# GpSimd keeps a running sum of the finished feature tiles for three layer-norm means of a two-layer backbone

## Chip, cores and metric

One core of a Trainium2 chip. The metric is the device time of one execution in microseconds (us). Engines are named as in the profile: PE (TensorE matmul), PEld (its weight load), DVE (VectorE), ACT (ScalarE), POOL (GpSimd), SP (SyncE, which issues most of the DMAs).

## The reference, cut to what matters

Two layers (DEPTH = 2) work on 512 latent and 128 context tokens of width 1024. Each layer is a mixer (attention and two recurrent groups) and then a channel mixer (SwiGLU in layer 0, top-2-of-8 experts in layer 1), each followed by a residual and a layer norm:

```
mix = mixer(...)                                  # ends in ... @ w_out[l]
x = layer_norm(alpha * x + g1 * mix, ln_g[l, 0], ln_b[l, 0])
x = layer_norm(alpha * x + g2 * channel_mixer(l, x * (1 + sc2) + sh2), ln_g[l, 1], ln_b[l, 1])

def layer_norm(x, g, b):
    mu = jnp.mean(xf, -1, keepdims=True)
    var = jnp.mean(jnp.square(xf - mu), -1, keepdims=True)
    return (xf - mu) * lax.rsqrt(var + NORM_EPS) * g + b
```

The change concerns `mu` in three of the four norms: after the mixer of layer 0, after the channel mixer of layer 0, after the mixer of layer 1. The last norm works on rows of tokens and is not touched.

## The kernel before, in words

The residual stream is held transposed in SBUF: `xT` has 128 partitions, KT = 8 feature tiles and NT = 640 tokens, float32, so `xT[:, m]` is one tile of 128 features x 640 tokens. The mean over features runs over partitions and over the eight tiles. PE makes it: a 128x128 matrix of the value 1/1024 (`mean`, a constant) times every tile, accumulated in one PSUM slot, which leaves the mean of each token in all 128 partitions. `average(i, k)` (line 2918) issues this for tile k of norm i: one call of `wide` (line 2330), a product of 512 and one of 128 columns; as these are float32, the trace shows two matmul instructions for each, four per tile. `variance(i)` (line 2927) does the same with the squared centred tiles, in four pieces of tokens.

**Norm 1 of each layer (mean1).** PE computes the output projection in eight parts wo0 to wo7 (`mixer`, lines 2891 to 2899), 48 f16 matmuls of 512 or 128 columns each. DVE adds each finished part to its tile of `xT` (line 2179, the stt helper at 1695, one instruction for the latent and one for the context columns), and frees the PSUM slot. Behind wo4 PE issues the mean's tiles 0 to 2, behind wo5 tile 3, behind wo6 tile 4 and behind wo7 tiles 5, 6 and 7 (lines 2938 to 2948). Each `average` waits for DVE's addition to that tile (`L.done`).

**Norm 2 of layer 0 (mean2).** The feed-forward network runs over 11 slabs of 256 hidden columns. In the last slab the second product `down(m, 1)` finishes output tile m, DVE adds it to `xT[:, m]` (line 2215). Behind tile 6 PE issues the mean's tiles 0 to 3, and behind tile 7 the tiles 4 to 7 (lines 2991 to 3002).

**Behind each mean.** DVE subtracts it in four pieces of tokens (line 1783), ACT squares (1473), PE sums the squares, ACT makes 1/sqrt (1453, 1454), DVE scales (1768), DVE and ACT modulate (1774, 1461), ACT and DVE split the result in two f16 halves (1467, 1780), and PE starts the next products piece by piece.

**GpSimd's order of work around the change.** POOL works through its own program in order: `lower` (line 827; the instruction is line 831) makes the low f16 half of a weight piece of 128x2048. In each layer the last of these are the four pieces wo0 to wo3 (lines 986 to 990); the stores of the new states go out behind wo1 (`send`, line 837). In layer 0 there follow the 11 slabs of `slab(i)` (line 995): three weight pieces each (line 1000) and two activation tiles (line 1003). Then layer 1 begins with `lower` of its pieces qa0 and qa1. SP fetches a weight piece into one of three buffers of `wbuf` when POOL has lowered the one before in it (lines 683 to 694 and 733). `out_done` counts the kernel's stores, six in each layer. `va` holds the value rows of the layer; its last part is a source of one of the stores (line 861).

Of the kernel before, what the change touches and what calls it, by code (L numbers as in the profile page):

```python
# [135 lines left out]
TURN_UNIT = {3: 2, 5: 3, 8: 4, 10: 5, 13: 6, 15: 7, 18: 8}  # L136
LAST_TURN = 9


# [149 lines left out]
def backbone_kernel(nc, x_prompt, x_sample, cache_k, cache_v, state_gdn, state_hgrn, c, c_ctx, w_mod, b_mod, w_in,  # L289
# [12 lines left out]
    with ctx:  # L302
# [153 lines left out]
        rsb = [mem(mix, 4 * CVW + CVW * i, CVW) for i in range(2)]  # L456
        vaf = va[:, :, :].rearrange("p t n -> p (t n)")
        osq, osqL, osqC = mem(spare, 0, 2, NT), mem(mix, 2048, 2, NT)[:, :, 0:LAT], mem(mix, 3328, 2, P)
        ors, orsL, orsC = mem(spare, 1280, NT), [mem(spare, 1280, LAT), vaf[:, 0:LAT]], mem(spare, 1792, 2, P)
# [5 lines left out]
        def mixed(i, k):  # L465
# [57 lines left out]
            "near_in wide_ready ltc_ready tt_ready t5_act t6_act ah_clear centred sq_ready rstd_ready scaled xn_ready v_in v_exp "  # L523
            "hot_ready m_hot g2_out zero_in id_ready x1_first x1_out picked_ready slots_ready tiles_ready gates_ready xs_out "
            "m_hi13 m_lo13 m_hi2 m_lo2 m_xt m_xhi m_xlo m_up m_silu m_act m_ahi m_alo m_turn m_at "
# [297 lines left out]
        def _(pool):  # L823
# [10 lines left out]
            def send(l, S, dst):  # L834

                for f in range(2):
                    pool.dma_start(heads_of(dst[0, l], f), head(S, f)).then_inc(sg["out_done"], 16)

            for l in range(DEPTH):
# [146 lines left out]
                for what in OUT_PIECES:  # L986
                    lower(l, what)
                    if what == "wo1":
                        L.done(f"{l}.hs4")
                        send(l, SH, new_sh)  # L990
                if l % 2:
                    continue
# [14 lines left out]
                L.made["w_lo"] = sbase + 3 * SLABS[l]  # L1007
                L.took["w_hi"] = sbase + 3 * SLABS[l]

            pool.wait_ge(sg["slots_ready"], 1)  # L1010
# [1297 lines left out]
        def _(pe):  # L2308
# [108 lines left out]
            for l in range(DEPTH):  # L2417
# [500 lines left out]
                def average(i, k):  # L2918

                    if i == 1:  # L2920
                        L.done(J(f"wo{k}"))
                    else:
                        pe.wait_ge(ps_free[k % 4], 3 * (SLABS[l] - 1) + base[k % 4] + 2 + k // 4)
                    s = ps[:, PS[J(f"mean{i}")][0]]
                    return wide(s, mean, xT[:, k], k == 0, k == KT - 1)

# [11 lines left out]
                for m in range(3, KT):  # L2938
                    open_(J(f"wo{m}"))
                    close(mixer(m, range(KT), lat + last), J(f"wo{m}"))  # L2940
                    if m == 4:
                        open_(J("mean1"))
                        for k in range(3):
                            average(1, k)
                    if m > 4:
                        average(1, m - 2)
                average(1, 6)
                close(average(1, 7), J("mean1"))
                variance(1)
# [4 lines left out]
                def slab(i, first=False, last=False):  # L2954
# [30 lines left out]
                    for m in range(KT):  # L2985
                        b = m % 4
                        if m >= 3:
                            pe.wait_ge(ps_free[b], i * 3 + (base[b] + 1 + m // 4))
                            down(m, 0)
                        down(m, 1).then_inc(ps_full[b], 1)  # L2990
                        if last and m == 6:
                            open_(J("mean2"))
                            for k in range(4):
                                average(2, k)

# [3 lines left out]
                slab(SLABS[0] - 1, last=True)  # L2999
                for k in range(4, KT):  # L3000
                    ins = average(2, k)
# [159 lines left out]
```

## Time and profile before

| | us |
|---|---|
| median of 3 runs | 2382.66 |
| lowest and highest of them | 2378.59, 2385.62 |
| span of the profiled execution (first to last instruction) | 2378.1 |
| PE busy in it | 2118.8 (89%) |
| DVE, ACT, POOL busy | 1449.5 (61%), 1283.3 (54%), 754.2 (32%) |

The profiled execution's own time is not listed apart from the three runs; its span stands 4.6 us under their median and 0.5 us under the lowest. A span leaves out what lies before the first and behind the last instruction. PE works nearly all the time, so a stage is to be read by what stands between its matmuls. A timeline row gives the start, the duration, the engine, the line, the operation, the output and input, the shape and the number of instructions merged in the row; in brackets the idle time of the engine before it and what ended it.

### The profile page before, as it was taken

To read this page: it belongs to the slowest core of one execution; us is meant where nothing else is said; L and a number is where in the kernel's file an instruction comes from. 1 tells how busy PE (TensorE), PEld (TensorE's weight loads), DVE (VectorE), ACT (ScalarE), POOL (GpSimd) and SP (SyncE) were. 2 spreads that over 40 slices of the span, in tenths; PEclk is the share of its full clock that TensorE was granted. 3 is DMA by queue.
4 is the path that set the end of the run, shared out by engine and by line. 5 is a ranking of instruction groups with operands and counts; after the bars stand their busy time and mean duration, and the time that the engine had idled before them with its cause. 6 is when DMAs were issued, how large, how long until landed. Compare 5 with 4: busy or idle time off the path is not lost.

```text
span 2378.1 us, 54636 instructions
## 1 busy us (share of the span) xinstructions
PE 2118.8 (89%) x23130; PEld 1305.1 (55%) x23130; DVE 1449.5 (61%) x1797; ACT 1283.3 (54%) x1665; POOL 754.2 (32%) x556
## 2 busy tenths in 40 slices
PE   5999787978989999999899878878869999999994
PEld 3756456745565555555675558645544444444442
DVE  3254656668261221215558667595379999999985
ACT  3443554556453333423543665465368877778763
POOL 0332115433404242423233236422023333333332
PEclk8999898988999999999999989998979999999997
DMA  9352680020303131315231000100456777990014
GB/s 285 121 174 77 212 285 28 4 58 8 106 17 106 53 106 53 106 53 166 77 103 39 1 10 4 41 21 22 140 223 223 238 265 276 330 335 34 36 65 183
DMA packets 215529, 278.48 MB, mean 117 GB/s; under 512 B 28321, under 2 KB 188941, under 8 KB 215183
## 3 DMA queue, kind: packets, MB, share of 16 engines
q1 hardware_dynamic: 203776, 243.60, 31.5%
q0 software_dynamic: 8432, 29.89, 3.4%
q8 instruction: 166, 2.72, 0.5%
q10 hardware_dynamic: 3103, 1.85, 0.3%
q14 instruction: 52, 0.43, 0.1%
HBM read 368.36 MB, written 29.11 MB: 167 GB/s over the span
## 4 chain that ended last, share of the span: by engine, by line
PE 53%; issue 16%; DVE 13%; POOL 8%; ACT 7%; DMA 2%; SPq 1%; POOLq 0%; DVEq 0%; ACTq 0%
PE ps L2328 50%; POOL mix L1000 6%; DVE mix L1695 1%; DVE arena L1687 1%; DVE mix L1687 1%; DMA wbuf<-in_w_mod 1%; POOL mix L1003 1%; DVE small L1910 1%; DVE arena L1691 1%; SPq L727 1%; DVE mix L1849 1%; DMA const<-in_w_mod 1%; ACT mix L1461 1%; PE ps L3097 1%; PE ps L3073 1%
## 5 line engine op out<-in xcount | busy, mean ns | idle before, releaser
L2328 PE MATMUL ps<-hT,mix 128*128 128x512 f16 (+2 forms) x3024 | 376.7, 287 | 25.0 <-DVE hT L1687 11.8
L2328 PE MATMUL ps<-w,xgT 128*128 128x512 f16 x1632 | 366.3, 381 | 5.3 <-DVE w L2228 5.3
L2228 DVE SCALAR_TENSOR_TENSOR w<-wst,w 128x2048 f16<-128x2048 f32 x136 | 309.8, 2318 | 25.6 <-ACT w L1558 25.5
L2328 PEld LDWEIGHTS ps<-hT,mix 128*128 128x128 f16 x3024 | 227.1, 99 | 172.9 <-issue 22.2
L1032 POOL TENSOR_TENSOR a<-aval,a 128x256 f16<-128x256 f32 x68 | 158.3, 2328 | 370.4 <-ACT a L1606 370.4
L2328 PEld LDWEIGHTS ps<-w,xgT 128*128 128x128 f16 x1632 | 157.7, 98 | 184.5 <-issue 9.6
L1558 ACT ACTIVATE w<-wst 128x2048 f16<-128x2048 f32 x136 | 251.5, 1898 | 9.6 <-DMA xs_rows<-htok,slot_i 9.6
L2328 PE MATMUL ps<-mix 128*128 128x512 f16 (+5 forms) x1856 | 204.7, 288 | 15.7 <-POOL mix L1003 8.8
L2328 PE MATMUL ps<-hT,arena 128*128 128x128 f16 (+1 forms) x1440 | 200.7, 300 | 1.1 <-DVE const L1687 1.1
L2328 PE MATMUL ps<-w2m,aT 128*128 128x512 f16 x816 | 187.2, 379 | 3.8 <-DVE aT L2266 3.8
L2328 PEld LDWEIGHTS ps<-mix 128*128 128x128 f16 (+3 forms) x1856 | 121.3, 123 | 90.4 <-POOL mix L1003 12.4
L2234 DVE SCALAR_TENSOR_TENSOR w2m<-wst,w2m 128x2048 f16<-128x2048 f32 x68 | 155.7, 2290 | 15.0 <-ACT w2m L1566 14.6
L2192 DVE SCALAR_TENSOR_TENSOR mix<-ps,mix 128x640 f32<-128x640 f32 x22 | 18.1, 825 | 238.6 <-PE ps L2328 238.6
L831 POOL TENSOR_TENSOR arena<-wbuf,arena 128x2048 f16<-128x2048 f32 x24 | 99.8, 4157 | 195.7 <-ACT arena L1063 195.6
L2328 PEld LDWEIGHTS ps<-hT,arena 128*128 128x128 f16 x1440 | 111.3, 98 | 88.0 <-issue 5.8
L1000 POOL TENSOR_TENSOR mix<-wbuf,mix 128x2048 f16<-128x2048 f32 x33 | 134.4, 4089 | 57.0 <-ACT mix L1510 56.8
L2328 PEld LDWEIGHTS ps<-w2m,aT 128*128 128x128 f16 x816 | 79.6, 98 | 100.2 <-DVE aT L2266 4.7
L1566 ACT ACTIVATE w2m<-wst 128x2048 f16<-128x2048 f32 x68 | 129.4, 1902 | 0.2 <-PE ps L2328 0.2
L2328 PE MATMUL ps<-arena 64*32 64x32 f32 (+5 forms) x4320 | 104.7, 219 | 22.0 <-issue 18.4
L1003 POOL TENSOR_TENSOR mix<-mix 128x640 f16<-128x640 f32 x22 | 30.7, 1396 | 256.8 <-ACT mix L1519 256.8
L2199 DVE TENSOR_TENSOR arena<-arena,ps 128x640 f32<-128x640 f32 x80 | 65.6, 821 | 73.7 <-PE ps L2328 73.7
L2328 PEld LDWEIGHTS ps<-arena 64*32 64x32 f32 (+3 forms) x4320 | 69.8, 116 | 54.1 <-issue 41.9
(359 smaller groups left out, 3546.3 us busy)
## 6 DMA issues: line engine op xcount, KB each, us to landing
wst<-in_moe_w SPq DMA_DIRECT2D x204, 1024.0 KB
wbuf<-in_w_mod SPq DMA_DIRECT2D x40, 1024.0 KB
wbuf<-in_ffn_w SPq DMA_DIRECT2D x33, 1024.0 KB
wbuf<-in_w_in SPq DMA_DIRECT2D x20, 1024.0 KB
xs_rows<-in_table SPq DMA_DIRECT2D x17, 512.0 KB, 6.4
ys_rows<-yb POOLq DMA_DIRECT2D x17, 512.0 KB, 4.2
wbuf<-in_w_out SPq DMA_DIRECT2D x32, 256.0 KB
xg<-xs_rows POOLq DMA_DIRECT2D x16, 512.0 KB, 5.5
```

The costliest lines, as they stand in the source:

```text
L727: sp.dma_start(o, i).then_inc(w_full[slot], 64 // len(parts))
L831: L.do(g.tensor_tensor(split_parts(what)[1], wpiece(WP[f"{l}.{what}"][0], n), split_parts(what)[0], ALU.subtract), "w_lo")
L1000: g.tensor_tensor(v[1], wpiece(j), v[0], ALU.subtract).then_inc(sg["w_lo"], 1)
L1003: g.tensor_tensor(a2[1][:, t], gbuf[:, t], a2[0][:, t], ALU.subtract).then_inc(sg["a_lo"], 1)
L1032: g.tensor_tensor(a16[:, s % 2, 1, :], aval[:, s % 2, :], a16[:, s % 2, 0, :], ALU.subtract).then_inc(sg["m_alo"], 1)
L1558: a.activation(quarter(s, p)[0], staged(s, p), ACT.Copy, scale=WS).then_inc(sg["m_hi13"], 1)
L1566: a.activation(w2p[s % 2][0], staged(s, 2), ACT.Copy, scale=WS).then_inc(sg["m_hi2"], 1)
L1687: ins = v_.tensor_tensor(o, x, y, op)
L2199: v_.tensor_tensor(yacc[:, m], yacc[:, m], ps[:, b, 0:NT], ALU.add).then_inc(ps_free[b], 1)
L2228: v_.scalar_tensor_tensor(out=q[1], in0=staged(s, p), scalar=WS, in1=q[0], op0=ALU.mult, op1=ALU.subtract).then_inc(sg["m_lo13"], 1)
L2234: v_.scalar_tensor_tensor(out=q[1], in0=staged(s, 2), scalar=WS, in1=q[0], op0=ALU.mult, op1=ALU.subtract).then_inc(sg["m_lo2"], 1)
L2328: return mm_(o, w, x, start=first, stop=last, skip_group_check=True)
```

## The change

A new buffer `xsum` of 128 x 640 float32 lies on `va`. In each layer, behind `lower(wo3)`, POOL waits for all stores of the layer (`out_done`) and for wo0, and then adds tile 1 to tile 0 into `xsum` and tiles 2 to 6 to it, each when DVE has finished that tile: six additions (SUM1 = 7). In layer 0, behind the 11 slabs, it does so again for tiles 1 to 5: five additions (SUM2 = 6). The last addition signals `sum_ready`. PE multiplies `xsum` first (`average_sum`) and then the tiles that the sum doesn't hold: tile 7 in mean1, tiles 6 and 7 in mean2, all behind the last part. The calls that stood between the parts are gone.

```diff
--- before.py
+++ after.py
@@ -135,6 +135,7 @@
 MOD_FETCH = {"f0": 0, "f1": 1, "b0": 2, "b1": 3, "b2": 4, "ba": 5, "i": 6, "gc": 7}
 TURN_UNIT = {3: 2, 5: 3, 8: 4, 10: 5, 13: 6, 15: 7, 18: 8}
 LAST_TURN = 9
+SUM1, SUM2 = 7, 6
 
 
 def mod_pieces(x):
@@ -455,6 +456,7 @@
         sqb = mem(mix, 0, 4, CVW)
         rsb = [mem(mix, 4 * CVW + CVW * i, CVW) for i in range(2)]
         vaf = va[:, :, :].rearrange("p t n -> p (t n)")
+        xsum = vaf[:, 0:NT]
         osq, osqL, osqC = mem(spare, 0, 2, NT), mem(mix, 2048, 2, NT)[:, :, 0:LAT], mem(mix, 3328, 2, P)
         ors, orsL, orsC = mem(spare, 1280, NT), [mem(spare, 1280, LAT), vaf[:, 0:LAT]], mem(spare, 1792, 2, P)
         oat = [mem(spare, 1024 + P * i, P) for i in range(4)]
@@ -521,7 +523,7 @@
             "eg_ready dm_in dm_exp kg_ready egl_ready kd_ready qg_ready cs_ready t_ready t_turned lt_ready "
             "hg_ready lp_hi lp_lo kk_exp kk_ready kw_ready qb_ready qe_ready ke_ready ac_ready ah_ready o_zero o_sq oc_ready oc_sq rs_ready o_ready "
             "near_in wide_ready ltc_ready tt_ready t5_act t6_act ah_clear centred sq_ready rstd_ready scaled xn_ready v_in v_exp "
-            "hot_ready m_hot g2_out zero_in id_ready x1_first x1_out picked_ready slots_ready tiles_ready gates_ready xs_out "
+            "sum_ready hot_ready m_hot g2_out zero_in id_ready x1_first x1_out picked_ready slots_ready tiles_ready gates_ready xs_out "
             "m_hi13 m_lo13 m_hi2 m_lo2 m_xt m_xhi m_xlo m_up m_silu m_act m_ahi m_alo m_turn m_at "
             "m_down m_yact m_ydve row_in xr_in dg_ready y_psum y_mul lnv_ready lnr_ready lnb_ready").split()}
         st_full = [sem(f"st_full{i}") for i in range(3 * MQ)]
@@ -988,6 +990,12 @@
                     if what == "wo1":
                         L.done(f"{l}.hs4")
                         send(l, SH, new_sh)
+                pool.wait_ge(sg["out_done"], OUTS * (l + 1))
+                L.done(f"{l}.wo0")
+                for m in range(1, SUM1):
+                    L.done(f"{l}.wo{m}")
+                    L.do(g.tensor_tensor(xsum, xsum if m > 1 else xT[:, 0], xT[:, m], ALU.add),
+                         "sum_ready" if m == SUM1 - 1 else None)
                 if l % 2:
                     continue
                 base, sbase = PS_BASE[l], SPLIT_BASE[l]
@@ -1006,6 +1014,11 @@
                     slab(s)
                 L.made["w_lo"] = sbase + 3 * SLABS[l]
                 L.took["w_hi"] = sbase + 3 * SLABS[l]
+                for m in range(1, SUM2):
+                    for b in ([0, 1] if m == 1 else [m]):
+                        pool.wait_ge(ps_free[b % 4], 3 * (SLABS[l] - 1) + base[b % 4] + 2 + b // 4)
+                    L.do(g.tensor_tensor(xsum, xsum if m > 1 else xT[:, 0], xT[:, m], ALU.add),
+                         "sum_ready" if m == SUM2 - 1 else None)
 
             pool.wait_ge(sg["slots_ready"], 1)
             pool.wait_ge(sg["zero_in"], 16 * MT)
@@ -2922,7 +2935,13 @@
                     else:
                         pe.wait_ge(ps_free[k % 4], 3 * (SLABS[l] - 1) + base[k % 4] + 2 + k // 4)
                     s = ps[:, PS[J(f"mean{i}")][0]]
-                    return wide(s, mean, xT[:, k], k == 0, k == KT - 1)
+                    return wide(s, mean, xT[:, k], False, k == KT - 1)
+
+                def average_sum(i):
+
+                    open_(J(f"mean{i}"))
+                    L.need("sum_ready")
+                    wide(ps[:, PS[J(f"mean{i}")][0]], mean, xsum, True, False)
 
                 def variance(i):
 
@@ -2938,14 +2957,10 @@
                 for m in range(3, KT):
                     open_(J(f"wo{m}"))
                     close(mixer(m, range(KT), lat + last), J(f"wo{m}"))
-                    if m == 4:
-                        open_(J("mean1"))
-                        for k in range(3):
-                            average(1, k)
-                    if m > 4:
-                        average(1, m - 2)
-                average(1, 6)
-                close(average(1, 7), J("mean1"))
+                average_sum(1)
+                for k in range(SUM1, KT):
+                    ins = average(1, k)
+                close(ins, J("mean1"))
                 variance(1)
                 if l % 2:
                     continue
@@ -2988,16 +3003,13 @@
                             pe.wait_ge(ps_free[b], i * 3 + (base[b] + 1 + m // 4))
                             down(m, 0)
                         down(m, 1).then_inc(ps_full[b], 1)
-                        if last and m == 6:
-                            open_(J("mean2"))
-                            for k in range(4):
-                                average(2, k)
 
                 slab(0, True)
                 with pe.Fori(1, SLABS[0] - 1) as s:
                     slab(s)
                 slab(SLABS[0] - 1, last=True)
-                for k in range(4, KT):
+                average_sum(2)
+                for k in range(SUM2, KT):
                     ins = average(2, k)
                 close(ins, J("mean2"))
                 variance(2)
```

## Rows read from the trace of the kernel before

**Rows 1.** Page: busy time of each engine, share of the span and instructions.

```profile
PE 2118.8 (89%) x23130; PEld 1305.1 (55%) x23130; DVE 1449.5 (61%) x1797; ACT 1283.3 (54%) x1665; POOL 754.2 (32%) x556
```

**Rows 2.** Groups that touch `xT` (duration ns min/median/max).

```profile
L2328 PE MATMUL ps<-xT,const x96: 272/434/648, 630.4 to 1702.7; 128*128 128x512 f32 x48, 128*128 128x128 f32 x48
```

**Rows 3.** Timeline, mean1 of layer 0, PE and DVE.

```profile
630.39 3.46 PE L2328 MATMUL ps<-xT,const 128*128 128x512 f32 x12
...
633.69 3.42 PE L2328 MATMUL ps<-hT,mix 128*128 128x512 f16 x24
...
648.13 1.14 DVE L1695 SCALAR_TENSOR_TENSOR xT<-ps,modT,xT 128x512 f32<-128x512 f32 x2 [6.52 <-PE ps L2328]
...
655.52 3.46 PE L2328 MATMUL ps<-xT,const 128*128 128x512 f32 x12
...
655.79 1.14 DVE L1695 SCALAR_TENSOR_TENSOR xT<-ps,modT,xT 128x512 f32<-128x512 f32 x2 [6.52 <-PE ps L2328]
...
659.09 6.05 DVE L1687 TENSOR_TENSOR xT<-xT,ps 128x1024 f32<-128x1024 f32 x4 [2.16 <-PE ps L2328]
```

**Rows 4.** Timeline, GpSimd, in the same stretch.

```profile
604.99 1.30 POOL L837 DMA_DIRECT2D out<-states  x2 [1.29 <-DVE states L1687]
...
626.18 4.07 POOL L831 TENSOR_TENSOR arena<-wbuf,arena 128x2048 f16<-128x2048 f32 x1 [3.85 <-ACT arena L1063]
640.12 12.23 POOL L1000 TENSOR_TENSOR mix<-wbuf,mix 128x2048 f16<-128x2048 f32 x3 [9.87 <-ACT mix L1510]
```

**Rows 5.** Timeline, mean2 of layer 0, all engines.

```profile
1110.30 3.10 DVE L2215 SCALAR_TENSOR_TENSOR xT<-ps,modT,xT 128x512 f32<-128x512 f32 x6 [3.33 <-PE ps L2328]
...
1114.61 8.22 POOL L831 TENSOR_TENSOR mix<-wbuf,mix 128x2048 f16<-128x2048 f32 x2 [5.39 <-ACT mix L1063]
...
1116.89 1.01 DVE L2215 SCALAR_TENSOR_TENSOR xT<-ps,modT,xT 128x512 f32<-128x512 f32 x2 [0.62 <-PE ps L2328]
...
1124.26 4.54 PE L2328 MATMUL ps<-xT,const 128*128 128x512 f32 x16
...
1128.91 6.05 DVE L1687 TENSOR_TENSOR xT<-xT,ps 128x1024 f32<-128x1024 f32 x4 [3.37 <-PE ps L2328]
```

**Rows 6.** Timeline, end of mean1 of layer 1.

```profile
1699.53 3.46 PE L2328 MATMUL ps<-xT,const 128*128 128x512 f32 x12
...
1703.10 6.05 DVE L1687 TENSOR_TENSOR xT<-xT,ps 128x1024 f32<-128x1024 f32 x4 [2.16 <-PE ps L2328]
```

**Rows 7.** GpSimd's additions and a like one of DVE (ns min/median/max).

```profile
L963 POOL TENSOR_TENSOR mix<-mix,extra x4: 1263/1268/1271, 514.3 to 1593.6; 128x512 f32<-128x512 f32 x4
...
L963 POOL TENSOR_TENSOR extra<-extra x6: 1264/1467/2182, 491.5 to 1605.7; 128x512 f32<-128x512 f32 x6
...
L1003 POOL TENSOR_TENSOR mix<-mix x22: 1393/1396/1403, 700.3 to 1107.8; 128x640 f16<-128x640 f32 x22
...
L2199 DVE TENSOR_TENSOR arena<-arena,ps x80: 820/821/823, 709.4 to 1080.1; 128x640 f32<-128x640 f32 x80
```

**Rows 8.** A small GpSimd addition of layer 1, timeline.

```profile
1618.90 0.46 POOL L956 TENSOR_TENSOR arena<-arena,mix 128x128 f32<-128x128 f32 x1 [3.79 <-ACT arena L1329]
```

**Rows 9.** A DVE group with both tensors in SBUF (ns min/median/max).

```profile
L1695 DVE SCALAR_TENSOR_TENSOR xT<-arena,modT,xT x16: 351/750/4039, 1080.8 to 1094.4; 128x512 f32<-128x512 f32 x8, 128x128 f32<-128x128 f32 x8
```

**Rows 10.** First use of GpSimd's slab 0, timeline of PE.

```profile
673.72 2.84 PE L2328 MATMUL ps<-hT,mix 128*128 128x128 f16 x48
```

**Rows 11.** Waits of SP's queue (us in total, times, longest).

```profile
SPq L734 <- POOL mix L1000: 392.6, 30, 63.7
SPq L781 <- DVE w L2228: 252.5, 119, 8.8
```

**Rows 12.** Windows, the three norm stages: length, PE busy, granted clock, DMA, GB/s.

```profile
659.00:686.50 27.50, 17.60 (x175) 1.00 0.00 1
1128.90:1157.50 28.60, 19.10 (x175) 0.94 0.10 39
1703.10:1731.20 28.10, 16.48 (x188) 0.78 0.91 313
```

## The prediction, made before the changed kernel ran

> **What bounds the kernel now.** I read the page first: PE is busy for 89% of the span, GpSimd for 32% [rows 1]. So float32 work taken off PE can pay, and GpSimd has room, but only where the two meet in time. The groups on `xT` give the object: 96 matmul instructions between 630.4 and 1702.7, four for each of 3 x 8 = 24 tile products [rows 2]. Then I read each site in order of time. What is to be seen: PE goes from the last f16 product of wo4 straight into the mean's tiles and back without a gap, so these tiles lie on PE's own path, and behind wo7 nothing runs on PE but tiles 5 to 7, for whose end DVE waits with the centring [rows 3]. Mean2 and layer 1 look alike [rows 5, 6]. Behind each mean comes a chain of DVE, ACT and PE in small pieces that starts when the mean is there, so an earlier mean starts the whole rest earlier.
>
> **The price of a tile.** Three tiles take from 630.39 to the next f16 matmul at 633.69, 3.30 us [rows 3]: 1.10 us each. The merged 16 instructions of four tiles at 1124.26 last 4.54 us and the 12 of three tiles 3.46 us [rows 5, 3]; the difference, 1.08, agrees. The change leaves 2 products (sum, tile 7) in each mean1 and 3 (sum, tiles 6 and 7) in mean2, 7 of 24. Removed: 17 x 1.10 = 18.6 us of PE. What is not got back is what PE then waits for.
>
> **Mean1 of layer 0.** Ahead of wo7's end five tiles go: 5 x 1.10 = 5.50 us. wo7's last matmul is issued just before 655.52, so before 650.02 now. The sum is multiplied to 651.12. Tile 7 needs DVE's addition, which is there 1.41 us behind that point (655.79 + 1.14 = 656.93 against 655.52) [rows 3]: at 651.43, so PE waits 0.3 us, a wait that was hidden behind tiles 5 and 6 before. From the start of the last tile to the centring it took 3.57 - 2 x 1.10 = 1.37 us; 651.43 + 1.37 = 652.8 against 659.09: a gain of 6.3 us. I take 6.2, with 0.1 for a weight load that the wait may expose.
>
> Is the sum there by 650.0? An addition of 128x640 float32 stands nowhere. From GpSimd's 128x512 float32 additions at 1.264 us [rows 7] and its 128x128 at 0.46 us [rows 8] the slope is 0.80/384 = 2.09 ns per column, so 640 columns give 1.264 + 0.27 = 1.53 us. Lower bound: 1.40, the 640-column subtraction that writes f16 [rows 7]. Upper bound: 2.182 at 512 columns, the slowest of its group [rows 7], by columns 2.73. I take 1.53, whose rows have this type, and 1.6 with the gap between two. GpSimd is free at 630.25 [rows 4]. The stores it must wait for were issued by 606.3 [rows 4], 24 us earlier; costed at nothing. Tiles 1 to 4 are added by about 636.7, tile 5 when wo5 is in, tile 6 when DVE has wo6: 648.13 + 1.14 - 4 x 1.10 = 644.9 (four tiles stood before it), so the sum stands at 646.4, 3.6 us early. Even at 2.73 it is early.
>
> **What is moved behind the additions.** GpSimd's lowering of slab 0 ran from 640.12 to 652.35 [rows 4]. It now starts at about 646.5 and ends at 658.7. It has two followers. PE uses its first piece at 673.72 before [rows 10], about 667.5 now, against 650.6: cover of 17 us. SP fetches slab 1 into the freed buffers 6 us later; its waits for GpSimd on this line, 392.6 us in 30, show it standing ready long before a buffer is free [rows 11], and slab 1 is wanted only behind the whole of slab 0. Both cost nothing. The third neighbour is DVE: its centring (652.8 to 658.9) now lies beside that lowering. DVE's scalar_tensor_tensor with both tensors in SBUF rose from a median of 0.75 to 4.04 us [rows 9] between 1080.8 and 1094.4, about the length of one lowering, which ran there; but with one operand in PSUM DVE kept 0.820 to 0.823 us over 80 instructions of the network's loop, where GpSimd lowers too [rows 7], and 1.01 us at 1116.89, inside GpSimd's 1114.61 to 1122.83 [rows 5]. The centring reads PSUM, so I cost it at nothing. The first operation with two SBUF tensors is the scaling, behind the centring's 6.05 us [rows 3]: 658.9 against GpSimd's end at 658.7. Cost 0, bounds 0 and 0.6 (if the additions run at 2.73 there is one more us of overlap at most).
>
> The Trainium skill (GPSIMD Engine Reference, Specifications) says the same as these rows: the SBUF interfaces are shared with VectorE, with contention where a DVE instruction has two SBUF inputs. The same page (Engine selection) speaks against the change, as it gives elementwise additions to VectorE, GpSimd being about twice slower; the rows make it 1.53 to 0.82, but the queue it is put in is idle.
>
> **Mean1 of layer 1.** The same rows: 3.57 us from 1699.53 to 1703.10 [rows 6]. No slab follows, GpSimd has nothing behind the additions until the routing. Gain 6.2 us.
>
> **Mean2.** (Times without the gain of layer 0.) The four tiles before `down(7)` go (4.40): its last matmul is out by 1124.26 - 4.40 = 1119.86. DVE finishes tile 1 at 1110.30 + 2 x 1.03 = 1112.4; DVE then stays ahead of GpSimd, whose five additions at 1.53, with a gap of 0.05 each, end at 1120.3. So here the sum is the late one, by 0.4 us, and with the exposed weight load PE starts it at 1120.4. Three products at 1.10 and the drain: before, 4.65 us passed from 1124.26 to 1128.91 for four tiles, so 3.55 for three: centring at 1124.0 against 1128.91 [rows 5]. Gain 4.9 us; bounds 5.5 (additions at 1.40, no wait) and about -0.3 (additions at 2.73: sum at 1126.0). GpSimd's next lowerings (qa0, qa1) move from 1114.61 to about 1120.4 and end at 1128.6; the scaling that reads two SBUF tensors comes at 1130. Their weights are wanted where the norm's first piece is done, in layer 0 14.6 us behind the centring's start [rows 3, 10], so at about 1138.6. Nothing lost.
>
> **Sum.** 6.2 + 4.9 + 6.2 = 17.3 us, 0.73%. The norm, the network and the experts follow in a chain; SP's fetches there wait for DVE and GpSimd [rows 11], not these for data, so they start earlier too. The span goes from 2378.1 to 2360.8. The span lies 4.6 us below the median of 2382.66; I carry the gain over: 2365.4.
>
> **Rivals.** (1) GpSimd's additions are slow, near 2.73 us. For: a group of the same type reaches it [rows 7]. Against: its median is 1.467 and the like group beside it never passes 1.271, and DVE has only PSUM-fed work in mean2. Mean2 then gives nothing: -12.1 us, 2370.6. Chance 0.08.
> (2) Work fed from PSUM does feel GpSimd at the new overlap, or the experts' stage is paced by its fetches so that layer 1's gain is lost. Loss up to 6.2 at the centring of layer 0 or in layer 1, and both together about 12: gain 5, 2377.5, within noise. Rows 7 and 11 speak against. Chance 0.05.
> (3) Slower: TensorE's clock. In the three norm stages the granted clock was 1.00, 0.94 and 0.78 [rows 12], so it does fall from 2.4 to 1.2 GHz when PE has worked in short bursts. The change takes dense products away just before. If the clock then stood at 1.2 GHz in all three stages, PE's 17.6 us of work per stage could take twice as long, up to 17.6 more each, 52.8 - 17.3: 2418. It decides from 5.8 us lost per stage on. Against: the stages differ by only 1.2 us in length (27.4 us from 659.09 to 686.5; 28.6; 28.1) although the clock differs [rows 12], and f16 products still fill PE up to each mean. Chance 0.03. The Trainium skill (TensorE: Matmul & The Clock Gate, HAM oscillation) warns of the same: idle gaps between bursts bring half rate. By it the gain would shrink most at mean2 and layer 1, where the windows already show a low clock.
> (4) The products weren't the bound at all and the time stays, 2382.7: chance 0.01; PE has no gap ahead of the centring.
>
> **How the numbers follow.** Forecast 0.83 at 2365.4. Its own spread: the three runs of before lie 4 below and 3 above their median; the costs add -0.6 and +2, the clock +-1.2. That gives 2360 to 2371; the range reaches on to rival (1) and stops at 2373. A measurement of this kernel tells from no change about 0.3%, 7.1 us; (0.83 + 0.08) gives faster 0.91; rivals 2 and 4 same 0.06; slower 0.03.
>
> **What would show it.** Of `xT` products 28 matmul instructions instead of 96. GpSimd: 17 additions of 128x640 at about 1.53 us. The centring of the three norms 6.2, then 6.2 + 4.9 = 11.1, then 17.3 us before its old place: at 652.9, 1117.8 and 1685.8. A wait of PE for GpSimd in mean2 alone. It is wrong if the additions exceed 1.6 us beside DVE, if a PSUM-fed DVE instruction is stretched, or if a norm stage gets longer than 28.6 us.

## The result, and the profile after

| | before | after |
|---|---|---|
| median, us | 2384.14 (4 runs, 2378.59 to 2386.36) | 2358.21 (4 runs, 2356.78 to 2360.95) |
| ratio, 95% interval | | 0.9898 [0.9876, 0.992] |
| span of the profiled execution, us | 2378.1 | 2355.1 (its own time 2356.96) |

The change makes the kernel 1.0% faster, 26 us by the medians. The forecast was 2365.4 with a range of 2360 to 2373: the side is right, the size is not, and the median lies 1.8 us below the range. One later execution of the kernel before took 7245.06 us and enters no figure here.

The page of the profile after, to be read beside [rows 1]:

```profile
PE 2102.1 (89%) x23062; PEld 1293.1 (55%) x23062; DVE 1449.9 (62%) x1797; ACT 1283.4 (54%) x1665; POOL 782.3 (33%) x573
```

PE has lost 68 matmuls and as many weight loads, GpSimd has gained 17 instructions and 28.1 us. The groups that read `xT` on PE and write `va` (where the sum lies) on GpSimd (duration in ns, min/median/max):

```profile
L2341 PE MATMUL ps<-xT,const x16: 272/434/696, 652.4 to 1681.4; 128*128 128x512 f32 x8, 128*128 128x128 f32 x8
...
L997 POOL TENSOR_TENSOR va<-va,xT x10: 1532/1540/1550, 633.0 to 1673.9; 128x640 f32<-128x640 f32 x10
L1020 POOL TENSOR_TENSOR va<-va,xT x4: 1537/1544/1553, 1109.0 to 1113.8; 128x640 f32<-128x640 f32 x4
```

16 matmuls on `xT` and 12 on the sum are the 28 foretold; an addition takes 1.54 us (1.53 foretold). Mean1 of layer 0 in the timeline, which answers to [rows 3, 4] (L2341, L1708 and L1700 are the helpers that were L2328, L1695 and L1687):

```profile
645.98 1.55 POOL L997 TENSOR_TENSOR va<-va,xT 128x640 f32<-128x640 f32 x1 [4.97 <-DVE xT L1708]
647.79 12.14 POOL L1008 TENSOR_TENSOR mix<-wbuf,mix 128x2048 f16<-128x2048 f32 x3 [0.26 <-POOL va L997]
650.94 1.30 PE L2341 MATMUL ps<-va,const 128*128 128x512 f32 x4
651.21 1.14 DVE L1708 SCALAR_TENSOR_TENSOR xT<-ps,modT,xT 128x512 f32<-128x512 f32 x2 [5.38 <-PE ps L2341]
...
652.41 1.35 PE L2341 MATMUL ps<-xT,const 128*128 128x512 f32 x4 [0.17 <-DVE xT L1708]
653.86 6.06 DVE L1700 TENSOR_TENSOR xT<-xT,ps 128x1024 f32<-128x1024 f32 x4 [1.51 <-PE ps L2341]
659.95 1.23 DVE L1700 TENSOR_TENSOR xT<-xT,mix 128x1024 f32<-128x1024 f32 x1
```

The sum is complete at 647.53, 3.4 us before PE takes it. PE then waits 0.17 us for tile 7. The centring lasts 6.06 us (6.05 before) although GpSimd lowers beside it from 647.79 to 659.93, and the scaling, the first operation with two SBUF tensors, starts at 659.95. Mean2, against [rows 5]:

```profile
1107.32 1.58 POOL L1020 TENSOR_TENSOR va<-xT 128x640 f32<-128x640 f32 x1 [3.29 <-DVE xT L2228]
...
1108.97 6.41 POOL L1020 TENSOR_TENSOR va<-va,xT 128x640 f32<-128x640 f32 x4
...
1115.53 1.32 PE L2341 MATMUL ps<-va,const 128*128 128x512 f32 x4 [0.68 <-POOL va L1020]
```

The five additions last from 1107.32 to 1115.38, and here PE does wait for them, 0.68 us (0.4 foretold). Mean1 of layer 1 repeats layer 0: PE starts on the sum at 1678.86, DVE on the centring at 1681.77, against 1703.10 in [rows 6].

**The span cut in stages.** The marks are the starts of the first addition of an output part to `xT` (wo0, down(0)) and of the three centrings, all rows of DVE's timeline. In us:

| profile | start to wo0, layer 0 | to centring 1 | to down(0) | to centring 2 | to wo0, layer 1 | to centring 3 | to end |
|---|---|---|---|---|---|---|---|
| before | 614.94 | 44.15 | 451.21 | 18.61 | 530.05 | 44.14 | 675.00 |
| after | 615.93 | 37.93 | 451.26 | 14.00 | 524.72 | 37.93 | 673.33 |
| gain | -1.0 | 6.22 | 0.0 | 4.61 | 5.33 | 6.21 | 1.7 |

The three stages with a mean give 17.04 us, close to the 17.3 worked out. But 5.3 us come from the mixer of layer 1 and 1.7 from the last stage, in which the change touches nothing. That is the question of the experiments.

### The profile page after: what moved, and what is told of

It reads as the page before. It is cut to its first block, busy times and chain, and to the rows that moved or that the text cites. A ratio compares the mean times of both kernels' runs of the same rounds, so it can differ in the third digit from the quotient of the medians.

```text
span 2355.1 us, 54537 instructions
## 1 busy us (share of the span) xinstructions
PE 2102.1 (89%) x23062; PEld 1293.1 (55%) x23062; DVE 1449.9 (62%) x1797; ACT 1283.4 (54%) x1665; POOL 782.3 (33%) x573
## 4 chain that ended last, share of the span: by engine, by line
PE 52%; issue 15%; DVE 14%; POOL 8%; ACT 7%; DMA 2%; SPq 1%; POOLq 0%; DVEq 0%; ACTq 0%
PE ps L2341 50%; POOL mix L1008 5%; DVE arena L1700 2%; DVE mix L1700 2%; DVE mix L1708 1%; DMA wbuf<-in_w_mod 1%; DVE small L1923 1%; POOL mix L1011 1%; DVE arena L1704 1%; SPq L729 1%; DVE mix L1862 1%; ACT mix L1474 1%; PE ps L3109 1%; PE ps L3085 1%; DMA const<-in_w_mod 1%
## 5 line engine op out<-in xcount | busy, mean ns | idle before, releaser
L2341 PE MATMUL ps<-hT,mix 128*128 128x512 f16 (+2 forms) x3024 | 376.4, 287 | 20.8 <-DVE hT L1700 10.6
L2341 PE MATMUL ps<-w,xgT 128*128 128x512 f16 x1632 | 366.2, 381 | 4.5 <-DVE w L2241 4.5
L2341 PEld LDWEIGHTS ps<-hT,mix 128*128 128x128 f16 x3024 | 226.9, 99 | 169.1 <-issue 17.9
L2341 PEld LDWEIGHTS ps<-w,xgT 128*128 128x128 f16 x1632 | 157.6, 98 | 183.6 <-issue 8.5
L2341 PE MATMUL ps<-mix 128*128 128x512 f16 (+5 forms) x1856 | 202.7, 285 | 14.5 <-POOL mix L1011 8.8
L2341 PE MATMUL ps<-hT,arena 128*128 128x128 f16 (+1 forms) x1440 | 200.9, 301 | 1.1 <-DVE const L1700 1.1
L2341 PE MATMUL ps<-w2m,aT 128*128 128x512 f16 x816 | 187.2, 379 | 3.8 <-DVE aT L2279 3.8
L2341 PEld LDWEIGHTS ps<-mix 128*128 128x128 f16 (+3 forms) x1856 | 119.8, 121 | 88.7 <-POOL mix L1011 12.4
L2341 PEld LDWEIGHTS ps<-hT,arena 128*128 128x128 f16 x1440 | 111.2, 98 | 88.6 <-issue 6.0
L2341 PEld LDWEIGHTS ps<-w2m,aT 128*128 128x128 f16 x816 | 79.6, 98 | 100.2 <-DVE aT L2279 4.7
L2341 PE MATMUL ps<-arena 64*32 64x32 f32 (+5 forms) x4320 | 105.9, 220 | 21.6 <-issue 17.9
L2341 PEld LDWEIGHTS ps<-arena 64*32 64x32 f32 (+3 forms) x4320 | 70.2, 116 | 54.2 <-issue 41.8
```

Source lines behind the costliest of these rows:

```text
L2341: return mm_(o, w, x, start=first, stop=last, skip_group_check=True)
```

## The experiments

Every kernel ran beside the kernel before on the same chip. The gain in the table at the end of this section is the mean of those runs of before minus the mean of the kernel's own.

**1 to 4: how much is noise, and whose gain is it.** The kernel before again, the changed kernel again, the change in the two mean1 alone, and in mean2 alone. Theory A says that only the three steps count and that the rest is the clock and the spread of the runs; theory B says that the change has a second effect somewhere else.

> The kernel before, unchanged, timed against itself. Theory A (the steps): the change is worth 17.0 us, the sum of the three shifts of the centring that the profile after shows (6.2, 4.6, 6.2), and the other 6 us of the 23 by which the spans differ are TensorE's clock, whose half-rate stretches fall on other work in each execution. Then this pair differs by nothing on average, but single executions and the two profiles differ by up to about 6 us, and the difference sits in stages with half-rate stretches, not in the network's loop. Theory B (a second effect of the change, in layer 1): two profiles of the kernel before agree within 1 to 2 us in every stage, and the 5.3 us that layer 1 gained come from the change.

> The changed kernel again, with more rounds. Theory A: 17 us faster, ratio 0.9929, with the centring of mean1 in layer 0 6.2 us nearer to the start of its part wo4, mean2's 4.6 us nearer, mean1's in layer 1 6.2 us nearer, and layer 1 between its first products and wo0 the same as before but for the clock. Theory B: 23 to 26 us faster, ratio 0.989 to 0.990, and layer 1 ahead of wo0 shorter by about 5 us in this profile too.

```diff
--- a3_mean1_only: mean2 as before, GpSimd adds nothing behind the slabs
-                for m in range(1, SUM2):
...
+                        if last and m == 6:
+                            open_(J("mean2"))
+                            for k in range(4):
+                                average(2, k)
...
-                average_sum(2)
-                for k in range(SUM2, KT):
+                for k in range(4, KT):
```

> Only the two mean1 use GpSimd's sum; mean2 is as before. Theory A: 2 x 6.2 = 12.4 us faster, ratio 0.9948. Theory B, if the second effect comes from these: up to 18 to 21 us faster.

```diff
--- a4_mean2_only: the two mean1 as before
-                for m in range(1, SUM1):
...
+                    if m == 4:
+                        open_(J("mean1"))
+                        for k in range(3):
+                            average(1, k)
+                    if m > 4:
+                        average(1, m - 2)
```

> Only mean2 uses GpSimd's sum, both mean1 are as before. Theory A: 4.6 us faster, ratio 0.9981. PE waits for the sum by 0.7 us as in the profile after. Theory B, if the second effect comes from this (it lies ahead of layer 1, where the 5.3 us appeared): 10 to 13 us faster.

Before again: 2380.01, ratio 0.9992 [0.998, 1.0003]. The whole change: 2359.82, 0.991 [0.9894, 0.9926]. Mean1 alone: 2364.08, 0.994 [0.9923, 0.9956]. Mean2 alone: 2371.62, 0.9968 [0.9956, 0.9981]. The stages with a mean repeat within 0.06 us wherever their form is the same. The two parts give 16.2 and 8.8 us, each some 4 more than its steps (12.4 and 4.6): the extra comes with either part, and is not their sum. What is new in both, and what is not?

**5 to 8: additions alone, removed products alone, the wait in mean2, layer 1 alone.**

```diff
--- b1_adds_only: GpSimd adds as in the changed kernel, PE multiplies all eight tiles
-                average_sum(1)
-                for k in range(SUM1, KT):
...
+                average(1, 6)
+                L.need("sum_ready")
+                close(average(1, 7), J("mean1"))
```

> The additions alone: TensorE multiplies all eight tiles in their old places, GpSimd issues the 17 additions all the same and its lowerings start as late as in the changed kernel; TensorE also waits for the sum ahead of tile 7, which is there by then. Theory A (the gain is what the three means give back, and the rest of the difference between runs is the start stage and the clock): no gain and no loss, ratio 1.000 with up to 0.0006 either way for the clock; the stages from wo0 to the centring stay at 44.15 and 44.15 us, the one from down(0) to mean2's centring at 18.61. Theory B (something common to every changed program, such as the later lowerings or the changed layout of the instructions, gives some 4 us by itself): ratio 0.998, 4 to 5 us faster with the same three stages unchanged. If the additions did cost something through shared memory, the stages beside them would be longer, by 0.1 us or more each.

```diff
--- b2_products_only: no additions, no wait for them; the mean leaves out tiles 1 to 6 (mean2: 1 to 5)
-                    L.need("sum_ready")
-                    wide(ps[:, PS[J(f"mean{i}")][0]], mean, xsum, True, False)
+                    wide(ps[:, PS[J(f"mean{i}")][0]], mean, xT[:, 0], True, False)
```

> The removed products alone: TensorE multiplies tile 0 in the place of the sum and then the last one or two tiles, GpSimd adds nothing and TensorE waits for no sum; the mean leaves out tiles 1 to 6 (1 to 5 in mean2), with the time of everything behind it unchanged. Theory A: the three stages shrink as in the changed kernel, by 6.22, 6.22 and in mean2 by 4.61 plus the wait of 0.68 for the sum, 5.3: in all 17.7 us, ratio 0.9926; GpSimd's lowering of slab 0 starts at about 640 and not 648 and is beside nothing of VectorE's norm. Theory B with the additions as its cause: the same 17.7 and nothing more. Theory B with another common cause: 21 to 22 us, ratio 0.991.

```diff
--- b3_tile6_first: order of the products of mean2
-                average_sum(2)
-                for k in range(SUM2, KT):
-                    ins = average(2, k)
+                open_(J("mean2"))
+                pe.wait_ge(ps_free[6 % 4], 3 * (SLABS[l] - 1) + base[6 % 4] + 2 + 6 // 4)
+                wide(ps[:, PS[J("mean2")][0]], mean, xT[:, 6], True, False)
+                L.need("sum_ready")
+                wide(ps[:, PS[J("mean2")][0]], mean, xsum, False, False)
+                ins = average(2, 7)
```

> The changed kernel with the order of mean2's products turned: TensorE takes tile 6 first, then the sum, then tile 7. Both theories: the wait of 0.68 us for GpSimd's sum lies beside tile 6's 1.1 us and is gone, the stage from down(0) to mean2's centring falls from 14.00 to about 13.4 us, the other stages stay. Against the kernel before 17.05 + 0.6 = 17.65 us by theory A (ratio 0.9926), about 22 by theory B (0.9908). Tile 6 itself is ready: VectorE adds tile 7 at the same time as TensorE starts, so no new wait is expected; if tile 6 were the late one, the stage would stay at 14.0.

```diff
--- b4_layer1_only: layer 0 as before
+                if l == 1:
+                    average_sum(1)
```

> One mean alone: only mean1 of layer 1 uses the sum (six additions, four products fewer ahead of the last matmul of wo7 than before, and two behind it); both means of layer 0 are as before. Theory A: 6.2 us, ratio 0.9974; the stage from wo0 to the centring of layer 1 is 37.93 and that of layer 0 44.15 us. The stage behind layer 1's centring tells whether its 1.3 us (673.3 us in the three profiles with the new mean, 674.4 to 675.0 in the three with the old) belong to this mean: with it 7.5 us, ratio 0.9969. Theory B: 10 to 11 us, ratio 0.9956.

Additions alone: 2381.48, ratio 1.001 [0.9996, 1.0023]; the 17 additions are in the trace (1.54 us), and no stage changes. GpSimd's later lowerings are worth nothing either way. Products alone, a kernel whose mean leaves out the tiles that the sum would hold: 2357.20, 0.9908 [0.989, 0.9926]. So the extra belongs to the products that PE no longer issues. Layer 1 alone: 2374.26, 0.9977 [0.9966, 0.9988]: 6.22 us at its mean and nothing extra, with the stage before it at 530.47 us. The extra needs a change in layer 0, *ahead* of that stage.

Tile 6 first: 2353.59, 0.9894 [0.9874, 0.9914]. Its rows of PE in mean2, three products end to end:

```profile
1108.58 1.30 PE L2341 MATMUL ps<-xT,const 128*128 128x512 f32 x4
1109.71 1.25 PE L2341 MATMUL ps<-va,const 128*128 128x512 f32 x4
1110.79 1.25 PE L2341 MATMUL ps<-xT,const 128*128 128x512 f32 x4
```

The wait is gone and the stage takes 13.14 us, 0.86 less than in the changed kernel (0.6 expected). The rest of its lead is within the spread of the runs.

**Where in the stage.** I laid the timelines of layer 1's mixer over each other, from centring 2 on. In two places, 454 and 473 us behind it, the profiles with layer 0 unchanged (before, its repetition, additions alone, layer 1 alone) fall back by 1.2 us each against the six others. In the kernel before, PE's rows there, from two stretches of its timeline:

```profile
1582.42 0.44 PE L2328 MATMUL ps<-mix 128*64 128x128 f32 x4
1582.79 0.43 PE L2328 MATMUL ps<-mix,states 64*64 64x128 f32 x4
1584.41 0.44 PE L2328 MATMUL ps<-mix 128*64 128x128 f32 x4 [1.19 <-issue]
...
1601.90 0.43 PE L2328 MATMUL ps<-arena,mix 128*64 128x128 f32 x2
1603.16 0.38 PE L2328 MATMUL ps<-arena,mix 128*64 128x128 f32 x2 [0.82 <-issue]
```

and the same products in the changed kernel:

```profile
1573.57 0.44 PE L2341 MATMUL ps<-mix 128*64 128x128 f32 x4
1573.94 0.44 PE L2341 MATMUL ps<-mix,states 64*64 64x128 f32 x4
1574.30 0.44 PE L2341 MATMUL ps<-mix 128*64 128x128 f32 x4
...
1591.85 0.44 PE L2341 MATMUL ps<-arena,mix 128*64 128x128 f32 x4
1592.22 0.44 PE L2341 MATMUL ps<-arena,states 64*64 64x128 f32 x4
```

Groups of four follow at a pitch of 0.37 us in both, but in the kernel before PE stands still in the middle of the run for 1.2 and 0.8 us, and the releaser is "issue": it waits for nothing that the profile shows. The second stall even cuts a group of four in two. What an engine can lack there is the instruction itself. The stretch from 1146 to 1646 of the kernel before has these rows, in the windows (PE and PEld busy with their counts come first) and among its DMA queues:

```profile
1146.00:1646.00 500.00, 430.00 (x7244) 310.28 (x7245) 335.01 (x485) 271.22 (x501) 176.15 (x182) 0.94 0.12 36
```

```profile
q8 instruction: 58, 0.95, 0.8%
```

58 packets of 0.95 MB / 58 = 16.4 KB bring 7244 + 7245 matmuls and loads, 250 instructions a packet, and 254 with the 230 semaphore and register instructions that the trace has for PE in this stretch. So TensorE's program comes in pieces of some 256 instructions, here mostly every 4 to 5 us where the products are small. The Trainium skill (Runtime: NRT & Kernel Launch, Instruction fetch mechanics) states the same piece, 16 KiB or 256 instructions, and calls its cost mostly hidden; these two rows show where it isn't. Each tile product taken out removes 8 instructions (four matmuls, four loads), so every piece behind it holds other instructions: 48 fewer behind mean1, 88 behind both means of layer 0, 40 with mean2 alone. This is theory C.

**9 to 12: shift the stream, change nothing else.** Padding of tiny products, behind mean2, whose result the first true product overwrites:

```diff
-                        L.need("sq_ready")
                         j = J(f"var{i}{'abcd'[v]}")
                         s = open_(j)
+                        if i == 2 and v == 0:
+                            for _i in range(22):
+                                mm(s[0:32, 0:32], mean[0:64, 0:32], mean[0:64, 0:32])
+                        L.need("sq_ready")
```

22 of them (88 instructions) or 11 (44) in the changed kernel, 42 (168) or 64 (256) in the kernel before. PE's wait for the squares moves behind the padding.

> The changed kernel with 88 tiny TensorE instructions (22 float32 products of 64x32 by 64x32, each two loads and two products) put where TensorE waits for VectorE's squares behind mean2; their result is overwritten. From there on TensorE's instructions stand at the same places of its stream as in the kernel before, up to the mean of layer 1 (11 products of 8 instructions had gone by then). Theory C (the second effect is TensorE's instruction fetch: it stalls in layer 1's mixer, 454 and 473 us behind mean2's centring, in the four profiles whose stream stands as before there, and does not in the six whose stream is 40 to 90 instructions shorter, and the last stage has 0.2 to 1.3 us of the same kind): both stalls are back, the stage from mean2's centring to wo0 of layer 1 is about 2.4 us longer than in the like profile of the changed kernel, the last stage is 674.4 and not 673.4 us, and of the gain over the kernel before 17 to 17.5 us are left, ratio 0.9928. Theory A (steps and clock alone): no stall depends on it, the ratio stays at that of the changed kernel's runs so far, 0.991, and no gap comes back. The 22 products themselves lie in a wait of 2.7 us or more and cost nothing in both.

> The same with 44 instructions (11 products): a control for what the padding costs by itself. The stream then stands 44 instructions short of before in the mixer of layer 1, where the stalls were absent (at 40 and 48), and 92 short in the last stage. Theory C and theory A: as the changed kernel, ratio 0.991, last stage 673.4 us, no gap at 454 and 473 us. If padding costs time by its execution, half of what the 88 cost.

> The kernel before, all products kept, with 168 such instructions (42 products) in the same wait. As a fetch brings 256 instructions, 168 more stand to its borders as 88 fewer do. Theory C: the two stalls of layer 1's mixer are gone although nothing was taken out, 2.4 us less there, and about 1 us less in the last stage: 3.5 us faster than the kernel before, ratio 0.9985, if the 42 products fit into the wait of 2.7 us; what sticks out of it is seen as a longer way from mean2's centring to the first square and is to be taken off. Theory A: nothing gained, ratio 1.000 or, if they stick out, above. A shift that did not wrap at 256 would leave the stalls or put them elsewhere.

> The kernel before with 256 padding instructions (64 products) instead of 168. Theory C: 256 more stand to the borders of the fetches as none, so both stalls of layer 1's mixer (454 and 473 us behind mean2's centring) are back, where 168 had removed them. The 64 products take about 4.3 us by the 2.84 us that 42 took, 1.8 us more than the 2.5 us between the last product of mean2 and the first of the squares; so the time is 0 to 2 us above the kernel before, ratio 1.0004 (0.9996 to 1.0012), against 0.9979 with 168. A rival by which any padding at this place helps, whatever its size (the clock, say, kept up by the tiny products), expects no stall at the two places and 0.998 or less.

Changed + 88: 2362.44, ratio 0.9922 [0.9908, 0.9935]. Changed + 44: 2358.18, 0.9903 [0.9885, 0.992]. Before + 168: 2375.72, **0.9979 [0.9969, 0.9988]**, a kernel that does more work and is faster. Before + 256: 2381.38, 1.0008 [0.9997, 1.002]. The first place in PE's timeline of changed + 88:

```profile
1573.18 0.44 PE L2341 MATMUL ps<-mix,states 64*64 64x128 f32 x4
1573.54 0.32 PE L2341 MATMUL ps<-mix 128*64 128x128 f32 x1
1574.18 0.44 PE L2341 MATMUL ps<-mix 128*64 128x128 f32 x3 [0.32 <-issue]
...
1591.66 0.43 PE L2341 MATMUL ps<-arena,mix 128*64 128x128 f32 x3
1592.92 0.32 PE L2341 MATMUL ps<-arena,mix 128*64 128x128 f32 x1 [0.82 <-issue]
```

of before + 168:

```profile
1580.90 0.44 PE L2328 MATMUL ps<-mix,states 64*64 64x128 f32 x4
1581.27 0.90 PE L2328 MATMUL ps<-mix 128*64 128x128 f32 x20
...
1598.08 0.44 PE L2328 MATMUL ps<-arena,mix 128*64 128x128 f32 x4
1598.45 0.43 PE L2328 MATMUL ps<-arena,states 64*64 64x128 f32 x4
```

and of before + 256:

```profile
1581.63 0.32 PE L2328 MATMUL ps<-mix 128*64 128x128 f32 x1
1582.29 0.44 PE L2328 MATMUL ps<-mix 128*64 128x128 f32 x3 [0.34 <-issue]
...
1599.78 0.43 PE L2328 MATMUL ps<-arena,mix 128*64 128x128 f32 x3
1600.76 0.32 PE L2328 MATMUL ps<-arena,mix 128*64 128x128 f32 x1 [0.55 <-issue]
```

Two quite different programs, one with 88 and one with 256 instructions of padding, stop at the same instruction of the same group of four, within one matmul of where the kernel before stops; with 168 neither place stops. The rival that any padding helps falls with the 256, and so does theory A, by which nothing depended on it. The idle time that the rows give for the first place is shorter than expected (0.32 and 0.34 us against 1.19); it is 0.33 and 0.73 us in additions alone and before again too. The 42 products of before + 168 took 2.84 us and held the squares up by 0.2 us. All kernels together:

| kernel | stream in layer 1's mixer against before | two stalls | mixer stage of layer 1, us | last stage, us | gain, us | from the mean stages alone |
|---|---|---|---|---|---|---|
| before | 0 | yes | 530.05 | 675.00 | | |
| before again | 0 | yes | 529.90 | 674.61 | 2.1 +-1.1 | 0 |
| additions alone | +2 | yes | 530.83 | 674.73 | -2.0 +-1.1 | 0 |
| layer 1 alone | 0 | yes | 530.47 | 674.40 | 5.2 +-1.1 | 6.2 |
| changed + 88 | 0 | yes | 531.28 | 674.18 | 18.5 +-0.8 | 17.0 |
| before + 256 | +256 | yes | 530.63 | 674.33 | -1.7 +-1.3 | 0 |
| changed | -88 | no | 524.72 | 673.33 | 24.8 +-2.0 | 17.0 |
| changed again | -88 | no | 528.25 | 673.25 | 21.3 +-1.5 | 17.1 |
| mean1 alone | -48 | no | 522.94 | 673.42 | 16.2 +-1.6 | 12.4 |
| mean2 alone | -40 | no | 525.23 | 674.44 | 8.8 +-1.5 | 4.6 |
| products alone | -90 | no | 528.18 | 673.48 | 22.9 +-1.1 | 17.9 |
| tile 6 first | -88 | no | 528.39 | 673.45 | 26.0 +-1.8 | 17.9 |
| changed + 44 | -44 | no | 522.05 | 673.38 | 24.0 +-2.1 | 17.0 |
| before + 168 | +168 (-88) | no | 523.57 | 674.44 | 5.5 +-1.1 | 0 |

(+- is the standard error of the difference of the means.) Take the last column off the gain, and -2.0 to 2.1 us are left in the five rows with stalls that have a gain, but 3.8 to 8.1 us, mean 5.7, in the eight without. So the times of all runs divide the kernels in the same two groups as the single profiles do.

**The fetches themselves.** The DMA records of the traces have each packet of queue q8. In the kernel before the last packets ahead of the two stalls end at 1583.04 and 1601.81, and PE goes on at 1584.41 and 1603.16: 1.37 and 1.35 us later. Over both places of all six profiles with stalls it is 1.19 to 1.48 us. Counted in PE's own records (matmuls, loads, semaphores), the two places lie 1024 instructions apart in each of the six, four times 256. So they stand at borders of the 256-instruction pieces, and with them the counts at the other borders are known. The changed kernel has seven borders between 453 and 479 us behind centring 2; PE passes them with pauses of at most 0.12 us, each 1.4 us or more behind the end of the last packet. It isn't free of such stalls: at later borders it has one of 0.41 us at 1601.43 and one of 1.77 us at 1613.32, 1.35 and 1.45 us behind a packet's end. What PE lacks at these places is the next piece of its program. The shift decides which of the small products stand at a border, and how early the packet for it has landed.

The mixer stage is 529.90 to 531.28 us with the stalls, mean 530.5, and 522.05 to 528.39 without, mean 525.4: 5.1 us, and the two groups do not overlap. The two stalls are 2.4 of them at most. A second part, 2.3 us, lies right behind. These rows are windows of the kernel before and of the changed kernel around the same pair of ACT instructions (PE, PEld, DVE, ACT, POOL, then the granted clock):

```profile
1617.00:1624.00 7.00, 7.00 (x115) 4.33 (x103) 4.61 (x5) 2.33 (x8) 0.46 (x1) 0.50 0.02 5
```

```profile
1606.50:1611.00 4.50, 4.50 (x160) 3.13 (x162) 4.33 (x6) 1.44 (x4) 0.46 (x1) 1.00 0.02 4
```

In the kernel before the clock stands at 0.50 there, the level of 1.2 GHz, and the way between the same two instructions of ACT is 7.1 us; it is 5.5 to 7.1 us in the six profiles with stalls and 4.1 to 4.2 us in all eight without. But the clock is not the whole of it. It is low there in four of the six: before, additions alone, layer 1 alone and changed + 88. In before again (5.5 us) and before + 256 (6.4 us) the granted clock is full up to the last 0.5 us or throughout, and PE has one more stall of the same kind, 1.31 and 1.87 us:

```profile
1623.36 1.09 PE L2328 MATMUL ps<-arena 64*32 64x32 f32 x82 [1.87 <-issue]
```

This row is of before + 256, 1.61 us behind the end of a packet. In the eight others a stall at this border, of 1.18 to 1.77 us, falls behind the two instructions of ACT. That the low clock in the four comes *from* the stalls just before was tried by no run and isn't shown.

The last stage takes 674.2 to 675.0 us in eight profiles and 673.3 to 673.5 in six. All six have a stream shorter by 93 to 139 instructions there; but before + 168, which should stand like 88 fewer, has 674.44. No other kernel stood at 88 fewer in that stage (the nearest have 93 fewer, fast, and 48 fewer, slow). That part of my expectation missed, and the cause of this 1 us stays open.

## Why the prediction was wrong in its number

**Right.** The product at 1.10 us, the addition at 1.53 (1.54), the sum early by 3.4 us in mean1 and late in mean2, PE's wait of 0.17 for tile 7 (0.3 foretold), 28 matmuls on `xT` and the sum. The gains at the three means: 6.22, 4.61 and 6.21, in all 17.04, against 6.2, 4.9 and 6.2. The order moved behind the additions cost nothing: the centring beside the lowering stayed at 6.06 us (1.01 us per pair of additions in mean2), and the run with the additions alone shows no loss. Rivals 1 and 2 are out by this, and rival 4. Rival 3, the clock in the norms, is out too: the stage from centring 1 to down(0) begins with a norm and took 451.26 against 451.21 us, and no stage behind a mean grew in the changed kernel. In two of the fourteen profiles that stage took longer, 453.25 us (changed + 44) and 452.34 us (before + 256), one with and one without the new mean ahead of it, so this does not go with the change.

**Mis-sized, mean2.** The sum was late by 0.68 and not 0.4 us, and the stage gave 4.61 and not 4.9. Counted from the first addition of DVE in the stage, GpSimd began 0.1 us later than worked out, and the five additions took 8.06 us against 7.90 ("with a gap of 0.05 each" is a pitch of 1.58, and it is 1.61). It is 0.3 us of the 26. The bound beside it is off as well: by its own terms a sum at 1126.0 gives 1126.0 + 3.55 = 1129.6 and a loss of 0.6 us, not 0.3.

**The step that failed: "I carry the gain over".** It has two parts. The base: the three runs of before had a median of 2382.66; the 77 later runs of this kernel have a mean of 2380.2. The profiled execution, span 2378.1 and, with the 1.8 us that the own time of the changed kernel's profile lies above its span, 2379.9, was the better base, and I set it aside: 2.4 us. (The runs of before beside the first runs of the changed kernel have a mean of 2383.3, so by those alone the base was sound; the split between the two parts is known to some 2 us.) And the rest of the span was taken to stay as it was. It did not: 2380.2 - 17.04 = 2363.2, while nine runs of the changed kernel have a mean of 2359.3, 3.9 us less; against the runs of before beside them it is 7.7 and 4.3 us. The forecast misses the mean of the nine by 6.1 us: 2.4 of base and 3.9 of shorter stages, less 0.3 for mean2. The runs showed in its place that the mixer of layer 1, 450 us behind the last edit of layer 0, gets 5.1 us shorter by the profiles, since its instructions stand elsewhere in the pieces in which TensorE's program is fetched. Undoing the shift alone takes the gain back to 18.5 +-0.8 us, and shifting alone gives 5.5 +-1.1 us.

**The range.** +-1.2 for the clock was too narrow. The start stage, the same in every kernel here, took 609.8 to 619.7 us. Windows of the repetition of the changed kernel and of tile 6 first:

```profile
0.00:619.73 619.73, 514.76 (x8345) 354.75 (x8346) 343.83 (x586) 300.00 (x536) 186.59 (x190) 0.92 0.39 122
```

```profile
0.00:609.84 609.84, 506.21 (x8345) 349.20 (x8346) 349.83 (x586) 299.99 (x536) 184.90 (x190) 0.95 0.40 124
```

8345 matmuls in both, but 9.9 us apart, with the granted clock at 0.92 and 0.95. So one span against one span (23.0 us between the two profiles) carries an error of some us either way; only stages that hold a full clock, as the three means do, can be compared to 0.06 us.

## What to carry to other kernels

Cut both spans at marks that lie around each edit, and read the gain there; what a stage without any edit gives or takes is a finding of its own. Removing or adding instructions on PE, whose program streams in, shifts everything behind it, and where many small instructions run back to back this can cost or give several microseconds far from the edit: a padding of as many idle-time instructions as were removed tells the two apart. Where the same sum can be had earlier, put the product that doesn't need it first: tile 6 ahead of the sum hides the wait of mean2 and gives 0.86 us more at its stage. That version has the lowest median measured here, 2353.59 us; that it leads the changed kernel by more than the 0.86 us isn't shown.

## What the runs showed of the hardware that was not expected

- TensorE stands still for 0.3 to 1.9 us in the middle of a run of small float32 products ("issue" as the releaser), at an instruction that depends on the count of instructions ahead of it: with 0, 2 and 256 more, or 88 fewer and 88 of padding, the two stalls of layer 1's mixer are there; with 40, 44, 48, 88 and 90 fewer and with 168 more they are not. At both places of the six profiles it goes on 1.19 to 1.48 us behind the end of a packet of its program.
- The kernel before with 168 instructions more is faster by 0.2% (ratio 0.9979 [0.9969, 0.9988]).
- GpSimd's lowering beside a VectorE operation fed from PSUM cost that operation 0.01 us of 6.05. The Trainium skill (GPSIMD Engine Reference, Specifications) limits the contention to VectorE's instructions with two SBUF inputs or in a 2-port mode; the trace agrees, and the runs did not put such an instruction beside an addition.
